# Stage boundaries of a three-layer transformer kernel: column sums in two parts, split weights in pieces, filler matmuls, and a shift carried as a column

## The reference

```python
def rms_norm(t, g):      # root mean square over the 1024 features
    return t * lax.rsqrt(jnp.mean(t * t, axis=-1, keepdims=True) + eps) * g

for i in range(DEPTH):                                   # DEPTH = 2, 272 tokens
    f = swiglu(rms_norm(h, ln_ffn1[i, 0]), ffn1_w_gu[i], ffn1_w_down[i])
    h = h + 0.5 * rms_norm(f, ln_ffn1[i, 1])
    hn = rms_norm(h, ln_mix[i, 0])
    m = short_conv_mixer(...) if i == 0 else diff_attention_mixer(...)
    h = h + rms_norm(m, ln_mix[i, 1])
    f = swiglu(rms_norm(h, ln_ffn2[i, 0]), ffn2_w_gu[i], ffn2_w_down[i])
    h = h + 0.5 * rms_norm(f, ln_ffn2[i, 1])
```

```python
hn = rms_norm_2(x, g_mix) * (1 + m1) + m0
x  = x + m2 * (attention branches(hn) @ w_out)
hn = rms_norm_2(x, g_ffn) * (1 + m4) + m3
x  = x + m5 * swiglu(hn, w_gate_up, w_down)
```

## Time and profile before

| | |
|---|---|
| median of 3 runs | 1582.45 us |
| profiled execution: time | 1587.77 us |
| profiled execution: span | 1586.0 us |
| TensorE busy, matmul | 1505.5 us (95%), 11846 instructions |
| VectorE busy | 1060.1 us (67%) |
| ScalarE busy | 684.1 us (43%) |
| weights and inputs read from HBM | 266.73 MB |

### The profile page before, as it was taken

One profiled execution on the slowest core, in us unless ns is written; L12 is line 12 of the kernel. 1 busy time (PEld: TensorE's weight loads), 2 busy tenths in 40 slices (PEclk: granted clock), 3 DMA queues, 4 the chain that ended last, 5 costly groups with the idle time before them and its releaser, 6 DMA issues. The chain is left out here.

```text
span 1586.0 us, 28878 instructions
## 1 busy us (share of the span) xinstructions
PE 1505.5 (95%) x11846; PEld 1478.0 (93%) x11846; DVE 1060.1 (67%) x1416; ACT 684.1 (43%) x806; POOL 14.6 (1%) x31
## 2 busy tenths in 40 slices
PE   5999989989999899999899889999799999989999
PEld 5999989989999899999888689999788989989999
DVE  5666777766667766676766567677867665686652
ACT  5434353354433544433445454443432535454431
POOL 0000000000000000000000000000000000000000
PEclk9999999999999899999899799999798999999999
DMA  8454645435456554457233126547343224445450
GB/s 314 165 183 182 243 156 186 161 135 209 166 183 229 191 197 175 160 204 272 108 133 107 54 85 234 197 175 266 145 160 133 80 107 168 152 173 199 170 201 28
DMA packets 38155, 269.11 MB, mean 170 GB/s; under 512 B 4240, under 2 KB 5392, under 8 KB 5680
## 3 DMA queue, kind: packets, MB, share of 16 engines
q1 hardware_dynamic: 33120, 240.31, 41.8%
q0 software_dynamic: 3792, 26.44, 4.6%
q10 hardware_dynamic: 1152, 1.05, 0.2%
HBM read 266.73 MB, written 1.05 MB: 169 GB/s over the span
## 5 line engine op out<-in xcount | busy, mean ns | idle before, releaser
L1616 ACT ACTIVATE w_hi<-raw_weights 128x2048 fp32r<-128x2048 f32 x228 | 434.9, 1911 | 388.0 <-PE ps L342 383.3
L878 DVE TENSOR_TENSOR w_lo<-raw_weights,w_hi 128x2048 fp32r<-128x2048 f32 x194 | 442.3, 2290 | 167.1 <-ACT w_hi L1616 166.6
L340 PE MATMUL ps<-x_hi,w_hi 128*128 128x272 f32 x1440 | 427.6, 297 | 30.0 <-DVE w_lo L878 15.3
L341 PE MATMUL ps<-x_lo,w_hi 128*128 128x272 f32 x1440 | 423.3, 294 | 0.0
L342 PE MATMUL ps<-x_hi,w_lo 128*128 128x272 f32 x1440 | 422.2, 293 | 0.0
L340 PE MATMUL ps<-x_hi_s,w_hi 128*128 128x256 f32 x1072 | 313.5, 292 | 13.1 <-DVE x_lo_s L1097 4.7
L340 PEld LDWEIGHTS ps<-x_hi,w_hi 128*128 128x128 f32 x1440 | 279.3, 194 | 32.6 <-DVE w_lo L878 15.3
L341 PE MATMUL ps<-x_lo_s,w_hi 128*128 128x256 f32 x1072 | 304.7, 284 | 0.0
L342 PE MATMUL ps<-x_hi_s,w_lo 128*128 128x256 f32 x1072 | 304.5, 284 | 0.0
L341 PEld LDWEIGHTS ps<-x_lo,w_hi 128*128 128x128 f32 x1440 | 278.9, 194 | 0.4
L342 PEld LDWEIGHTS ps<-x_hi,w_lo 128*128 128x128 f32 x1440 | 278.2, 193 | 0.0
(11 more groups left out here) (227 smaller groups left out, 1824.4 us busy)
## 6 DMA issues: line engine op xcount, KB each, us to landing
raw_weights<-w_units SPq DMA_DIRECT2D x228, 1024.0 KB, 4.8
mod_w<-mod_units POOLq DMA_DIRECT2D x24, 1024.0 KB, 5.1
h<-x_in SPq DMA_DIRECT2D x1, 1088.0 KB, 5.2
out<-h ACTq DMA_DIRECT2D x8, 128.0 KB, 1.8
con<-constants POOLq DMA_DIRECT2D x1, 592.0 KB, 8.2
tab<-tables POOLq DMA_DIRECT2D x1, 512.0 KB, 3.5
f<-constants POOLq DMA_DIRECT2D x1, 136.0 KB, 8.4
vec<-vectors SPq DMA_DIRECT2D x1, 100.5 KB, 2.1
```

The source lines that it names most:

```text
L340: pe.matmul(dst, wh, hi, start=start, stop=False)
L341: pe.matmul(dst, wh, lo, start=False, stop=False)
L878: dve.tensor_tensor(w_lo[:, u % RING, :], raw[:, u % RING, :], w_hi[:, u % RING, :].bitcast(F32), ALU.subtract).then_inc(S["lo_ready"], 1)
L1616: act.activation(w_hi[:, u % RING, :], raw[:, u % RING, :], ACT.Copy).then_inc(S["hi_ready"], 1)
```

## The change

**Column sums in two parts.** On VectorE the sum of squares ends one slab earlier in `tail` (`last=6`). `column_sums_split` multiplies sq_sum by ones, and then the last square itself (sq[:, 1]), into the same PSUM columns. The sums go to banks of the old stage, the spread to the side bank as before.

**f and the pieces of weight.** f is copied out of PSUM by VectorE, line by line between its additions. ScalarE in return converts w_hi of a third unit in quarters after the squares 0, 1, 3 and 5 (`high_piece`). VectorE does one more whole unit of w_lo before the tail (`split_to(nx.u0 + 2)` in place of `+ 1`), and two quarters of the third beside root and spread, in place of two halves of the second.

**Order of the update.** h of a slab follows its pair_a directly; the addition of squares is moved between the two.

**First pass on x_hi alone.** Group 0 does for k = 0 the two passes that need only x_hi for all four tiles, then the four with x_lo.

**Fillers.** `keep_busy` issues matmuls of the bf16 identity with the mask, 272 columns, whose result nobody reads: 5 behind the column sums and 13 behind the spread; 60 and 10 behind the two spreads of w_in.

**Mod sums** come in pairs of columns after k = 0 to 5 of group 0, and between the slabs of w_in's small first group. The gains of w_in are computed before the tail.

**up 4** is made like the other up stages: x = h x gain, divided at eviction. The shift is added as columns: x_hi and x_lo get two more columns (257 and 258) that hold m3, all matmuls of up 4 have 258 columns, and column 257 of each tile is the shift's product, added as a bias in Silu and in a scalar_tensor_tensor.

**Layout.** a_hi and a_lo have a pitch of 272 tokens instead of 320; the region that they lie in gets 832 bytes smaller, and all that is allocated behind it moves. The load of the rope tables no longer waits for the last mod part.

up 4 follows w_out directly. The diff, cut to its core:

```diff
...
+N_SHIFTED = 190
...
+        self.cols = SEQ + 2 if name == "gate_up" and plan["u"] > N_SHIFTED else tokens
...
+                        hi_first = x_base is not None and k == 0 and st.u0 > 0
+                        if hi_first:
+                            pe.wait_ge(S["x_hi_ready"], x_base + 1)
+                            for m in range(GROUP):
+                                t = st.t0 + GROUP * g + m + (4 if st.name == "w_in" else 0)
+                                wait_bank(st, t, 8 * i)
+                                if bank_busy is not None:
+                                    bank_busy(m)
+                                hi_passes(ps[:, st.bank(t), 0:st.cols], u % RING, m * P, xs[0][:, 0, 0:st.cols])
                         if x_base is not None:
                             pe.wait_ge(S["x_ready"], x_base + k + 1)
-                        for m in range(GROUP):
+                        if hi_first:
+                            for m in range(GROUP):
+                                t = st.t0 + GROUP * g + m + (4 if st.name == "w_in" else 0)
+                                pe.matmul(ps[:, st.bank(t), 0:st.cols], w_hi[:, u % RING, m * P:m * P + P],
+                                          xs[1][:, 0, 0:st.cols], start=False, stop=False)
...
+            def column_sums_split(T, bank):
+                pe.wait_ge(S["sumsq_ready"], c.up("sumsq_ready"))
+                for n, at_token in enumerate(starts(T)):
+                    pe.matmul(ps[:, bank + n, 0:1], sq_sum[:, at_token:at_token + P], ones[:, 0:1], start=True, stop=False)
+                pe.wait_ge(S["sq_ready"], c.up("sq_ready", KT))
+                for n, at_token in enumerate(starts(T)):
+                    ins = pe.matmul(ps[:, bank + n, 0:1], sq[:, 1, at_token:at_token + P], ones[:, 0:1],
+                                    start=False, stop=True)
+                ins.then_inc(S["stats_done"], 1)
+            def keep_busy(st, nx, n):
+                bank = 0 if nx is stages["qkv"] else st.bank(st.t0 + 3)
+                for _ in range(n):
+                    pe.matmul(ps[:, bank, 0:TOK], ident_b[:, :], mask[:, :], start=True, stop=True)
...
-            def stats(T, bank, evict=True):
+            def stats(st, nx, evict=True, filler=13):
                 if evict:
-                    pe.wait_ge(S["f_ready"], c.up("f_ready", 8))
-                column_sums(T, bank)
-                spread(T, bank)
+                    pe.wait_ge(S["f_ready"], c.up("f_ready", 5))
+                column_sums_split(nx.T, st.bank(st.t0))
+                keep_busy(st, nx, 5)
+                if evict:
+                    pe.wait_ge(S["f_ready"], c.up("f_ready", 3))
+                spread(nx.T, side_bank(nx))
+                keep_busy(st, nx, filler)
...
-                    between[3] = [lambda: mod_sums(part, mod_bank(st))]
+                    for k in range(6):
+                        job = (lambda columns: lambda: mod_sums(part, mod_bank(st), columns))(range(2 * k, 2 * k + 2))
+                        between[k] = [job] + between.get(k, [])
...
-            stats(SEQ, 7)
-            mod_sums(3, 6)
-            stats(SEQ, 7, evict=False)
+            stats(stages["down", 3], w_in, filler=60)
+            stats(stages["down", 3], w_in, evict=False, filler=10)
...
+                    if 1 <= k < 7:
+                        mod_sums(3, 6, range(2 * k - 2, 2 * k))
...
-            stats(SEQ, side_bank(stages["up", 4]), evict=False)
-            gate_up(4, X0["up", 4], deferred=False)
...
+            def low_piece(n):
+                u, first = nxt[0], quarters[0]
+                quarters[0] = (first + n) % 4
+                cols = slice(first * UNIT // 4, (first + n) * UNIT // 4)
+                if first == 0:
                     dve.wait_ge(S["hi_ready"], u + 1)
                 ins = dve.tensor_tensor(w_lo[:, u % RING, cols], raw[:, u % RING, cols],
                                         w_hi[:, u % RING, cols].bitcast(F32), ALU.subtract)
-                if half == 1:
+                if first + n == 4:
                     ins.then_inc(S["lo_ready"], 1)
                     nxt[0] += 1
...
+                dve.tensor_tensor(gate, ps[:, b:b + 2, 0:C], bcast(rstd, C), ALU.mult).then_inc(S["tile_evicted"], 2)
...
+            def shift_columns(shift):
+                dve.wait_ge(S["shift_ready"], 1)
+                dve.tensor_tensor(x_lo[:, :, SEQ:SEQ + 2], shift.unsqueeze(2).broadcast_to([P, KT, 2]),
+                                  x_hi[:, :, SEQ:SEQ + 2].bitcast(F32), ALU.subtract)
+            def tail(st, gain, nx, next_gain, shift=None, normed=True):
                 T = st.T
                 off = TOK - T
-                split_to(nx.u0 + 1)
+                split_to(nx.u0 + 2)
                 if normed:
                     for m in range(8):
-                        add_square(m, T)
-                    squares_done()
-                    low_half()
-                    root(T, between=lambda: low_half())
-                update_and_prepare(T, off, gain, next_gain, shift, normed, nx, spread=ps[:, side_bank(nx), :], part=part,
+                        add_square(m, T, last=6)
+                        dve.wait_ge(S["sq_ready"], c.now("sq_ready") + m + 1)
+                        dve.tensor_copy(f[:, m, 0:T], ps[:, st.bank(st.t0 + m), 0:T]).then_inc(S["f_ready"], 1)
+                    squares_done(last=6)
+                    c.up("f_ready", 8)
+                    low_piece(1)
+                    dve.wait_ge(S["f_ready"], c.now("f_ready"))
+                    root(T, between=lambda: low_piece(1))
+                update_and_prepare(T, off, gain, next_gain, shift, normed, nx, spread=ps[:, side_bank(nx), :],
                                    src=None if normed else st)
...
+            def second_gains(w):
+                gains = gain2[:, 8 * w:8 * w + 8]
+                chain(dve.tensor_scalar(gains, mod[:, 8 + 24 * w:16 + 24 * w], 1.0, None, ALU.add))
+                chain(dve.tensor_tensor(gains, gains, vec[:, V_GMIX + 8 * w:V_GMIX + 8 * w + 8], ALU.mult))
+            def update_and_prepare(T, off, gain, next_gain, shift, normed, nx, update=True, spread=None, src=None, between=None):
                 n_h = c.now("h_ready")
                 n_v = c.now("vec_chain")
...
+                last = 7 if deferred else 6
+                hi, lo = x_of(nx)
                 for m in range(8 + 2):
+                    if update and m < 8 and normed:
+                        if m >= 2:
+                            dve.wait_ge(S["h_ready"], n_h + m - 1)
+                        dve.tensor_tensor(pair_a[:, m % 2, 0:T], f[:, m, 0:T], spread[:, 0:T], ALU.mult)\
+                           .then_inc(S["vec_chain"], 1)
+                        c.up("vec_chain")
+                    if m >= 2 and nx is not None:
+                        add_square(m - 2, T, last)
                     if update and m < 8:
                         if normed:
+                            scaled = pair_a[:, m % 2, 0:T]
+                            dve.wait_ge(S["vec_chain"], n_v + m + 1)
+                        else:
+                            scaled = ps[:, src.bank(src.t0 + m), 0:T]
+                            dve.wait_ge(S["tile_done"], src.t0 + m + 1)
+                        dve.scalar_tensor_tensor(h[:, m, off:off + T], scaled, gain[:, m:m + 1], h[:, m, off:off + T],
+                                                 ALU.mult, ALU.add).then_inc(S["h_ready"], 1)
                     k = m - 1
+                    if 0 <= k < 8 and deferred:
+                        dve.wait_ge(S["x_hi_ready"], c.up("x_hi_ready"))
+                        dve.scalar_tensor_tensor(lo[:, k, 0:T], h[:, k, off:off + T], next_gain[:, k:k + 1],
+                                                 hi[:, k, 0:T].bitcast(F32), ALU.mult, ALU.subtract)\
+                           .then_inc(S["x_ready"], 1)
...
             gate_up(3)
             down(3, mod_part(3))
             w_in = stages["w_in"]
-            tail(stages["down", 3], g_out[:, 24:32], w_in, gain2[:, 0:8], shift=mod[:, 0:8], part=3)
+            second_gains(0)
+            tail(stages["down", 3], g_out[:, 24:32], w_in, gain2[:, 0:8], shift=mod[:, 0:8])
             def rotation(dst, which, x, r=None):
...
-            tail(w_out, mod[:, 16:24], stages["up", 4], gain2[:, 8:16], shift=mod[:, 24:32], normed=False)
-            before_evictions(stages["up", 4], deferred=False)
+            second_gains(1)
+            shift_columns(mod[:, 24:32])
+            tail(w_out, mod[:, 16:24], stages["up", 4], gain2[:, 8:16], normed=False)
+            before_evictions(stages["up", 4])
...
+            def high_piece():
+                u, first = nxt[0], quarters[0]
...
+                cols = slice(first * UNIT // 4, (first + 1) * UNIT // 4)
+                ins = act.activation(w_hi[:, u % RING, cols], raw[:, u % RING, cols], ACT.Copy)
+                quarters[0] = (first + 1) % 4
+                if quarters[0] == 0:
```

(15 more changed lines are left out.)

225 lines of the change are left out of this document (97 added, 128 removed).

## The result

The changed kernel takes **1563.82 us**, the median of four runs (1561.02 to 1564.83); the kernel before took 1581.95 beside it (1581.13 to 1583.11). The ratio is 0.9872, 95% interval 0.9854 to 0.9891. Two more groups of runs gave 0.9868 (0.9841 to 0.9896) and 0.9885 (0.9863 to 0.9908). The forecast was 1565.0, the range 1553 to 1577. The mean of all 15 runs of the changed kernel is 1563.9.

A forecast was written before the change was run, and what follows sets the result against it. TensorE was taken to bound the kernel, busy 95% of the span, with gains only at seven stage boundaries. Terms summed to 20.0 us, less 3.0 for the clock: 17 off 1582.45 gives 1565 us, range 1553 to 1577.

The forecast's parts named there:

- w_in: Boundary down 3 to w_in: VectorE's extra weight unit delays the start; 3.5 us lost, bounds 2 gained to 6 lost.
- up 4: Boundary w_out to up 4: the root leaves the path, 6.7 us gained; shift columns cost 1.6; net 5.1 us.
- The stall: Five boundaries with a normalised update: the wait before the new stage's first matmul gets 1.1 to 1.6 us shorter.
- The clock: Boundaries other than w_in: assumed to stay up, less two half-clock stretches of 1.5 us each, 3 us in all.
- the signs named: At w_in, right: TensorE idle over 3 us; wrong: first matmul no later after down 3's last than 17.5 us.
- rival C: Five starts and w_in: fillers issued at 1.2 GHz hold up what is behind them; slower, 1593 us; chance 0.06.
- the layout: New pitch and moved addresses: 0 taken; bounds: up 3 loses 4.6 us, the a-matmuls win or lose 2.
- B: Fillers don't hold the clock: half-clock stretches stay at the three mod boundaries; 1573 us; chance 0.16.
- a sign named for wrong: Fillers taking over 200 ns each would show the forecast wrong.
- D: Streaming rate gets worse: up 3 goes to 117.4 ns, up 4 to 121; 1572 us; chance 0.09.

## Why the prediction was right, step by step

From the old stage's last matmul to the end of the new stage (w_in: to its long run), before less after, in us:

| boundary | forecast | three traces of the changed kernel |
|---|---|---|
| conv_in | 5.2 | 3.3, 3.5, 5.0 |
| up 1 | 0.8 | 0.8, 0.6, 0.7 |
| up 2 | 5.5 | 4.3, 5.2, 5.5 |
| qkv | 6.0 | 5.5, 5.5, 5.3 |
| up 3 | 0.9 | 1.0, 1.1, 1.1 |
| w_in | -3.5 | -0.3, -0.5, -0.3 |
| up 4 | 5.1 | 4.6, 4.6, 4.6 |
| sum | 20.0 | 19.2, 20.0, 21.9 |

*Right.* Where VectorE paced group 0 before (up 1, up 3) little is gained, and with the clock up the other three end it by VectorE and TensorE alike. The stall is 0.9 to 1.6 us shorter where no low stretch falls into it (5.5 to 5.8 us at conv_in, up 1, up 2 and qkv; 1.1 to 1.6 forecast). Up 4 gains 6.4 us of stall and gives 1.8 back by its rate.

*The clock.* The allowance of 3.0 us for two stretches that stay was right as to their number (one or two per trace at conv_in, up 1 or up 2, up to 1.7 us each), but the measured sums hold them already and reach 20: the terms above them were 2 to 3 us too small in all, w_in's by itself. For qkv the prediction says that its clock was the lowest but one; by the earlier trace rows it is the lowest but two (0.77, behind 0.64 and 0.76).

*Mis-sized: w_in.* The wait for the column sums is there as worked out (the first copy of f directly behind the unit, w_in's start 1.8 us later by it), but I had the fillers and the sums at half clock, the spread 6.8 us behind down 3's last matmul and 1.4 us of fillers on the path. The spread comes after 3.9 us, and the fillers bring the clock back while they wait for nothing. The loss was 0.3 to 0.5, not 3.5. Of the signs named, w_in's first matmul came barely later (17.9 us against 17.5), and TensorE's idle time of over 3 us did not come: it is 1.84. Without fillers this boundary loses 13 us: that is rival C's place, with the opposite cause. Fillers are not what makes it slow, their absence is.

*Mis-sized: the layout.* I took 0, with 2 us either way for the down stages. Taken back in whole it costs 3.7 us. The traces show 0.9 us for each of down 0 to 2 and 3.5 for down 4. Down 3 keeps nothing (63.9 us; 528 x 113 ns would be 59.8): TensorE waits 2.29 us for w_lo at 1101.25, VectorE being held by the last part of the mod vector and that by its load, and a low stretch follows.

*Missed: the start.* The first matmul comes at 15.91 instead of 15.33, and down 0 starts 1.0 to 1.9 us later. In the loop that makes the first x, the first weight unit's w_lo is called at slab 5; with the update's new order one more x_lo stands in front of it, so it starts at 13.57 instead of 12.99. That this is the cause is read from the order and not tested (VectorE, changed kernel):

```profile
13.15 0.50 DVE L1123 SCALAR_TENSOR_TENSOR x_lo<-h,vec,x_hi 128x272 fp32r<-128x272 f32 x1 [1.68 <-ACT x_hi L1760]
13.57 2.29 DVE L927 TENSOR_TENSOR w_lo<-raw_weights,w_hi 128x2048 fp32r<-128x2048 f32 x1
```

*Luck.* The total came within 1.2 us of the forecast though its terms did not: w_in was put 3 us too low and the layout about 4, the start was left out, and the 3 us held back for the clock were already in the measured sums. The mechanism was right at six of the seven boundaries; that the total fits so closely is partly chance.

*Rivals.* B (fillers don't hold the clock) fell: they do, and alone they are worth 10.7 us in the old order. But its sizes fit the kernel without fillers: 2.5 us at each mod boundary and 1.7 for up 1 and up 3 together, where that trace gains 3.7, 3.3, 2.8 and 1.2. C came true in small at conv_in, where 13 fillers at half clock take 213 ns each, a sign named for wrong, and make the stall 7.16 us, longer than the 6.32 of before; conv_in with its stall takes 83.8, 83.7 and 82.2 us with fillers and 83.4 with none; at the other starts and at w_in it fell. D was the wrong way round: the rate of 272 columns went up, and 256 columns with k outside have two rates, of which the new layout allows the better one. The rate of up 4, 121 at worst, is 120 ns. The 113 ns of up 3 are the least that any trace here shows for 256 columns; the 109.2 of the Trainium skill (TensorE: Matmul & The Clock Gate, "Back-to-back issue gap"), which that section gives for a matmul by itself and not for a stream, are reached nowhere.

What stays open: the parts add up to more than the 18.6 us between the medians (some 20 for the boundaries, 4 by the runs or 6 by the traces for the layout, less 1 to 2 at the start). All of it is set against one trace of before, an execution 5.3 us above its median, and there is no second. The shorter chain of the stall (sums in two parts, the order of the update, the first pass on x_hi) was never taken back by itself; what it is worth is read from the traces.

## What to carry to other kernels

Where a matmul engine stalls for several microseconds, try cheap matmuls in the wait. In the old order they alone were worth 10.7 us, while the five stalls got shorter by about 6 in all by the new order; they have to end before their successor's input is there, which 13 of them at half clock did not. One-column work spread in pairs between full matmuls was followed by no low stretch where the clock was up (0 of 9, against 4 of 6 blocks), but its worth in time is not shown, and where the clock is low already (w_in without fillers) it was no remedy. After any change of the memory layout look at the spacing of matmuls in every stage: 1.8 ns of 127 were worth 3 us by the traces, and nothing in the code showed it.
